# Hybrid encoder trunk, two layers: sums of squares as two rounded passes, and where squares and up-projection lifts stand

## The reference

```
h = rms_norm(x);  p = h @ W_in
A: 4 heads, two softmax maps each, RMS norm of every 64-wide q and k, partial rotary,
   w = softmax1 - lam * softmax2;  o = rms_norm(w @ v, subln_w) * (1 - lambda_init)
B: 4 q heads, 2 kv heads of 128, RMS norm of q and k, axial rotary
C: latent attention: cq (384) and ckv (256) normed, projected up to q (128 + 64 rotary per head),
   k (128 per head) and v; norms of q and k parts; one rotary key kr (64) shared by the heads
D: 4 pooling windows minus token, per-group linear, scale
y = concat(A, B, C, D) * silu(gates);  x = x + y @ W_out
```

## Time and profile before

| | us |
|---|---|
| median of 3 runs | 913.04 (912.84 to 913.1) |
| the profiled execution | 912.77 |
| its span in the trace | 911.0 |
| PE busy | 899.7 (99%) |
| DVE busy | 637.0 (70%) |
| ACT busy | 585.5 (64%) |

### The profile page before, as it was taken

The page is one execution under the profiler, slowest core; times in us unless marked ns, Lnnn a source line. Parts: engine busy times, 40 slices in busy tenths (PEclk is TensorE's granted clock), DMA queues, the critical chain, the costliest instruction groups (busy, mean ns, idle before and its releaser), DMA issues.

```text
span 911.0 us, 18111 instructions
## 1 busy us (share of the span) xinstructions
PE 899.7 (99%) x7054; PEld 858.4 (94%) x7054; DVE 637.0 (70%) x1071; ACT 585.5 (64%) x1045; POOL 0.2 (0%) x4
## 2 busy tenths in 40 slices
PE   8999999999999999999999999999999999999998
PEld 7998998999999999999999989999999999999998
DVE  7785887768777776766665658876687667666552
ACT  7678756678666667745554588566686666675331
POOL 0000000000000000000000000000000000000000
PEclk9999999999999999999999999999999999999999
DMA  8654343343444343445455544334425344445562
GB/s 332 260 188 142 134 142 132 109 139 129 140 141 142 138 148 128 145 149 192 166 195 185 186 155 169 119 119 161 158 93 186 128 151 145 149 171 185 187 201 78
DMA packets 22997, 143.83 MB, mean 158 GB/s; under 512 B 2560, under 2 KB 4736, under 8 KB 6528
## 3 DMA queue, kind: packets, MB, share of 16 engines
q1 hardware_dynamic: 22768, 142.64, 44.0%
q10 hardware_dynamic: 144, 0.04, 0.0%
HBM read 140.57 MB, written 2.10 MB: 157 GB/s over the span
## 4 chain that ended last, share of the span: by engine, by line
PE 89%; ACT 7%; DVE 2%; issue 1%; DMA 1%; SPq 0%; ACTq 0%; DVEq 0%
PE dense L725 25%; PE dense L727 24%; PE dense L726 24%; PE s_ps L889 4%; PE o_ps L924 4%; ACT w_hi L1014 2%; PE norm_ps L845 2%; PE t_ps L905 2%; DVE w_lo L1319 1%; ACT qw L1087 1%; DMA x<-xt_dram 1%; PE swap_ps L860 0%; ACT sq L1084 0%; PE norm_ps L727 0%; PE swap_ps L727 0%
## 5 line engine op out<-in xcount | busy, mean ns | idle before, releaser
L725 PE MATMUL dense<-h_hi,w_hi 128*128 128x272 f32 (+2 forms) x1440 | 427.1, 297 | 1.5 <-DVE h_lo L1299 0.9
L727 PE MATMUL dense<-h_hi,w_lo 128*128 128x272 f32 (+2 forms) x1440 | 412.6, 287 | 0.0
L726 PE MATMUL dense<-h_lo,w_hi 128*128 128x272 f32 (+2 forms) x1440 | 410.6, 285 | 0.0
L1319 DVE TENSOR_TENSOR w_lo<-raw,w_hi 128x1024 fp32r<-128x1024 f32 (+1 forms) x257 | 313.3, 1219 | 88.4 <-ACT w_hi L1014 82.3
L1014 ACT ACTIVATE w_hi<-raw 128x1024 fp32r<-128x1024 f32 (+1 forms) x257 | 271.3, 1056 | 68.7 <-PE dense L727 53.9
L725 PEld LDWEIGHTS dense<-h_hi,w_hi 128*128 128x128 f32 x1440 | 271.3, 188 | 8.2 <-issue 3.8
L726 PEld LDWEIGHTS dense<-h_lo,w_hi 128*128 128x128 f32 x1440 | 271.5, 189 | 1.3
L727 PEld LDWEIGHTS dense<-h_hi,w_lo 128*128 128x128 f32 x1440 | 271.1, 188 | 0.0
L725 PE MATMUL dense<-y_hi,w_hi 128*128 128x272 f32 (+1 forms) x500 | 143.1, 286 | 2.3 <-ACT q_st L1059 1.3
L727 PE MATMUL dense<-y_hi,w_lo 128*128 128x272 f32 (+1 forms) x500 | 142.7, 285 | 0.0
L726 PE MATMUL dense<-y_lo,w_hi 128*128 128x272 f32 (+1 forms) x500 | 142.4, 285 | 0.0
(11 more groups left out here) (161 smaller groups left out, 813.4 us busy)
## 6 DMA issues: line engine op xcount, KB each, us to landing
raw<-w_stream_dram SPq DMA_DIRECT2D x128, 1024.0 KB, 4.8
out_dram<-x SPq DMA_DIRECT2D x8, 256.0 KB, 6.3
x<-xt_dram SPq DMA_DIRECT2D x3, 544.0 KB, 8.9
raw<-w_stream_dram SPq DMA_DIRECT2D x3, 512.0 KB, 7.5
con<-consts_dram SPq DMA_DIRECT2D x1, 984.0 KB, 7.4
x<-xt_dram SPq DMA_DIRECT2D x2, 272.0 KB, 4.8
raw<-w_stream_dram SPq DMA_DIRECT2D x2, 256.0 KB, 4.6
d_w<-consts_dram SPq DMA_DIRECT2D x2, 256.0 KB, 5.1
```

The source lines that it names most:

```text
L725: nc.tensor.matmul(ps, whi, xhi, start=first, stop=False)
L726: nc.tensor.matmul(ps, whi, xlo, start=False, stop=False)
L727: return nc.tensor.matmul(ps, wlo, xhi, start=False, stop=last)
L1319: signal(nc.vector.tensor_tensor(w_lo[:, g % RING, 0:n], raw[:, e % RAW, CHUNK * half:CHUNK * half + n], w_hi[:, g % RING, 0:n].bitcast(F3 ...
```

## The change

It does six things.

1. The sums of rope_stat and sub_stat are made as two fp32r matmuls (`two`) into the same bank, of a rounded tile sq_hi and of what the rounding leaves, sq_lo, with rounded copies of the two tables (ones and blocks, exact in them; made once on ACT).
2. For a single tile ACT writes sq_hi as a third instruction of rope_pre or a second of sub_pre, and DVE gets a new stage sq_low (one subtraction). For a pair, DVE's sq_sum gets two more instructions, a copy (CAST) and a subtraction. PE waits for DVE's `summed` in every case.
3. For single tiles of aq and ak, for kr and for the sub norm, the sum and what follows it stand a slot later. Pairs' sums keep their slot, as do those of qr; kr's squares stand a slot later too. sub_slot avoids the slots in which A's and B's sums now stand.
4. On ACT rope_pre goes from 0.11 to 0.62 of the slot, behind p_out (0.56) and the lifts (0.6); on DVE the sums of pairs go from 0.2 to 0.64, behind pool, s_scale and rescale.
5. Up-projection tiles are lifted as stages of their own: the second tiles of the first three up chunks come behind the next split (up_next, 0.715), and the split of chunk 18 is pulled nearly a slot forward by `MOVED`, ahead of the rounding of the latent (y_hi).
6. Some small stores change place (eps, one, lambda and its sums, in stat, v_st; the sub weights in par), and stat is used with fewer columns.

```diff
 AT_SCALAR = dict(rope_fin=-0.166, ..., sub_fin=0.1, rope_pre=0.62,
...
+                 lift=0.6, up_out=0.705, up_next=0.715, split=0.71, x_square=0.72, y_gate=0.73, y_lat=0.74, ...)
+AT_VECTOR = dict(sq_sum=0.64, sq_low=0.64, lat_sum=0.2, rope_mid=0.25, ...
...
+MOVED = {..., **{("split", l, 18): -0.98 for l in range(DEPTH)},
...
                 if kind in ("aq", "ak"):
                     at(s, ("rope_pre", l, kind, i0 + j, j))
-                    at(s, ("rope_stat", l, kind, i0 + j))
-                    at(s + 1, ("rope_fin", l, kind, i0 + j))
+                    at(s, ("sq_low", "rope", l, kind, i0 + j))
+                    at(s + 1, ("rope_stat", l, kind, i0 + j))
+                    at(s + 2, ("rope_fin", l, kind, i0 + j))
...
-        at(s + 8, ("rope_pre", l, "kr", 0, None))
-        at(s + 9, ("rope_stat", l, "kr", 0))
-        at(s + 10, ("rope_fin", l, "kr", 0))
+        at(s + 9, ("rope_pre", l, "kr", 0, None))
+        at(s + 9, ("sq_low", "rope", l, "kr", 0))
+        at(s + 10, ("rope_stat", l, "kr", 0))
+        at(s + 11, ("rope_fin", l, "kr", 0))
...
-            at(s + 4 + c, ("up_out", l, c))
+            for j in range(UP_TILES[c]):
+                at(s + 4 + c, ("up_next" if c < 3 and j else "up_out", l, c, j))
...
-                at(s, ("sub_stat", l, n))
-                at(s + 1, ("sub_fin", l, n))
-                at(s + 1, ("y_split", "sub_fin", l, n))
+                at(s, ("sq_low", "sub", l, n))
+                at(s + 1, ("sub_stat", l, n))
+                at(s + 2, ("sub_fin", l, n))
+                at(s + 2, ("y_split", "sub_fin", l, n))
...
+        def two(ps, table, hi, lo):
+            nc.tensor.matmul(ps, table, hi, start=True, stop=False)
+            return nc.tensor.matmul(ps, table, lo, start=False, stop=True)
...
         def rope_stat(l, key, i):
-            if key in PAIRED:
-                pe.wait_ge(summed, sum_no[("rope", l, key, i)])
-            else:
-                pe.wait_ge(pre_done, pre_no[("rope_pre", l, key, i)])
+            pe.wait_ge(summed, sum_no[("rope", l, key, i)])
             norm_free("rope_stat", l, key, i)
-            sums = nc.tensor.matmul(norm_ps[:, t0:L], halves, sq[:, 2 * parity("rope_stat", l, key, i), t0:L],
-                                    start=True, stop=True)
+            half = parity("rope_stat", l, key, i)
+            sums = two(norm_ps[:, t0:L], halves_r, sq_hi[:, half, t0:L], sq_lo[:, half, t0:L])
...
         def rope_pre(l, key, i, j):
...
+            link(nc.scalar.activation(sq[:, 2 * half, t0:L], src, ACT.Square))
+            link(nc.scalar.activation(qw[:, half, t0:L], src, ACT.Copy, scale=pcol(l, key)))
+            signal(nc.scalar.activation(sq_hi[:, half, t0:L], sq[:, 2 * half, t0:L], ACT.Copy),
+                   pre_done, pre_no[("rope_pre", l, key, i)])
...
         def sq_sum(what, l, key, i=None):
...
-            signal(nc.vector.tensor_tensor(a, a, b, ALU.add), summed, n)
+            link(nc.vector.tensor_tensor(a, a, b, ALU.add))
+            high = sq_hi[:, half, t0:L]
+            link(nc.vector.tensor_copy(high, a))
+            signal(nc.vector.tensor_tensor(sq_lo[:, half, t0:L], a, high.bitcast(F32), ALU.subtract), summed, n)
+
+        def sq_low(what, *of):
...
+            signal(nc.vector.tensor_tensor(sq_lo[:, half, t0:L], sq[:, 2 * half, t0:L],
+                                           sq_hi[:, half, t0:L].bitcast(F32), ALU.subtract), summed,
+                   sum_no[(what, *of)])
```

More of the change, by code:

```diff
@@ L215, in make_plan @@
             at(s, ("rope_pre", l, key, i, None))
-            if key in PAIRED:
-                at(s, ("sq_sum", "rope", l, key, i))
+            at(s, ("sq_sum" if key in PAIRED else "sq_low", "rope", l, key, i))
             at(s + 1, ("rope_stat", l, key, i))
@@ L289, in build @@
     sq = sb("sq", [128, 4, L])
+    sums_of = sb("sums_of", [128, 256], F32R)
+    sq_hi = sb("sq_hi", [128, 2, L], F32R)
+    sq_lo = sb("sq_lo", [128, 2, L], F32R)
     qw = sb("qw", [128, 2, L])
@@ L303, in build @@
     lam_in = v_st[:, 0, 0:DEPTH * 256]
-    lam_sum = sb("lam_sum", [128, DEPTH * 2])
-    neg_lam = sb("neg_lam", [128, DEPTH])
-    sub_w = sb("sub_w", [128, DEPTH])
-    eps_c = sb("eps_c", [128, 1])
-    one_c = sb("one_c", [128, 1])
+    lam_sum = v_st[:, 1, 0:DEPTH * 2]
+    neg_lam, eps_c, one_c = stat[:, 2:2 + DEPTH], stat[:, 6:7], stat[:, 7:8]
     dense = [bank("dense0"), bank("dense1")]
@@ L914, in pv @@
             if branch == "c":
-                pe.wait_ge(up_taken, UP_TILES * (l + 1))
+                pe.wait_ge(up_taken, sum(UP_TILES) * (l + 1))
             else:
@@ L928, in sub_stat @@
         def sub_stat(l, n):
-            pe.wait_ge(pre_done, pre_no[("sub_pre", l, n)])
+            pe.wait_ge(summed, sum_no[("sub", l, n)])
             norm_free("sub_stat", l, n)
             t0 = first_query(l)
-            nc.tensor.matmul(norm_ps[:, t0:L], ones, sq[:, 2 * parity("sub_stat", l, n), t0:L],
-                             start=True, stop=True).then_inc(stat_done, 1)
+            half = parity("sub_stat", l, n)
+            two(norm_ps[:, t0:L], ones_r, sq_hi[:, half, t0:L], sq_lo[:, half, t0:L]).then_inc(stat_done, 1)
         run = dict(setup=warm_up, chunk=chunk, xsum=xsum, rope_stat=rope_stat, lat_stat=lat_stat, v_turn=v_turn, mix=mix,
@@ L985, in lambda_exp @@
             signal(nc.scalar.activation(lam_sum[:, :], lam_sum[:, :], ACT.Exp), lam_exp, 1)
+            act.wait_ge(s_const, 16)
+            nc.scalar.activation(sums_of[:, :], con[:, CC["ones"]:CC["ones"] + 256], ACT.Copy).then_inc(ones_ready, 1)
         def x_tile(l, kt):
@@ L1104, in sub_pre @@
             buffers_free("sub_stat", l, n)
-            signal(nc.scalar.activation(sq[:, 2 * parity("sub_stat", l, n), t0:L], o_ps[:, t0:L], ACT.Square), pre_done,
+            half = parity("sub_stat", l, n)
+            link(nc.scalar.activation(sq[:, 2 * half, t0:L], o_ps[:, t0:L], ACT.Square))
+            signal(nc.scalar.activation(sq_hi[:, half, t0:L], sq[:, 2 * half, t0:L], ACT.Copy), pre_done,
                    pre_no[("sub_pre", l, n)])
@@ L1182, in s_exp @@
                 signal(nc.scalar.activation(probs[0:nq, k % 2, m, :], s_ps[m][0:nq, 0:L], ACT.Exp,
[L1183 removed]
+                                            bias=stat[0:nq, m:m + 1], scale=SCALE[b],
                                             accum_out=stat[0:nq, 4 + m:5 + m]), exp_done, 2 * k + m + 1)
```

94 lines of the change are left out of this document (48 added, 46 removed).

## The result

The changed kernel takes 917.59 us (median of 6 runs, 916.92 to 917.82) against 912.94 for the kernel before (6 runs, 912.7 to 913.11): ratio 1.005, 95% interval 1.004 to 1.006. It is slower by 4.6 us where 909.7 was forecast, and lies outside the range.

A forecast was written before the change was run, and what follows sets the result against it. PE, busy 899.7 of 911.0 us, was taken as the bound. 912.77 less 9.1 for cheaper sums, less 7.2 for waits that go, plus 13.0 for waits that come gave 909.5 (909.7 as median), range 901 to 916.5.

The forecast's parts named there:

- The sums' price: On PE, two rounded passes take 0.252 us instead of 0.454 per sum; 44 sums save 9.1 us.
- The waits that go: PE's 11 waits on late ACT instructions, such as up-projection lifts and p_t copies, vanish with their restarts, saving 7.2 us.
- The three places: Three least-margin places where PE would newly wait on longer DVE and ACT chains: 2.7, 3.4 and 4.3 us.
- kn1: Second latent key pair (slot 30.6): its sum comes late behind the softmax's scale, 1.6 and 1.8 us, together 3.4.
- head 1: Differential head 1's product with the values waits for o_ps, held by the sub norm's last step: 1.8 and 2.5 us.
- kn0: First latent key pair (slot 24.6): its sum waits for DVE's subtraction, 1.1 and 1.6 us, together 2.7.
- Waits that come: New PE waits, since every sum now waits for DVE, which like ACT works in order: 13.0 us, bounds 4 and 19.
- "smaller" places: Margins under 0.5 us: query rope sum, c2's turn (0.3 a layer each), B's query pairs 0.8, late lifts 0.6; 2.6 us.
- The first (few waits): Rival: the new waits mostly don't come, as ACT and DVE have 30% spare; 4.5 us of waits, 901.2; 22%.
- the second: Rival: DVE falls behind on w_lo in the lead-in and differential heads, so dense chunks wait; 916; 16%.
- The third (passes no cheaper): Rival: a weight reload or switch eats the two passes' 0.20 us on PE; without the 9.1, 918.8; 4%.
- something else: Remaining rival: a clock that drops in a longer stall, or an order misread; mostly slower; 6%.

The follow-up runs named there:

- e1: Kernel before with only the up-projection's part: its tiles lifted as stages of their own, chunk 18's split pulled forward; 911.15 us (0.9979).
- e12: e1 with kr's square and scaled copy on ACT moved behind v_st's lifts; 911.97 us (0.9989).
- e9: Changed kernel's order of stages with the arithmetic of the kernel before: one fp32 sum, nothing added on ACT or DVE; 911.30 us (0.9981).
- e5: Changed kernel with the sub norm's last step, which frees o_ps, moved on DVE ahead of two rescales and s_max; 923.92 us (1.0114).
- e2: Changed kernel with each sum one fp32 matmul; ACT and DVE still make sq_hi and sq_lo, and PE waits for them; 920.03 us (1.0077).
- e13: e9 plus ACT's part of the addition alone: 30 copies to sq_hi that nobody reads; 913.01 us (1.0001).
- e14: e9 plus DVE's part alone: 30 subtractions, and copy and subtraction for 14 pairs, with PE waiting for DVE; 918.0 us (1.0055).
- e4: Changed kernel with squares on ACT back at 0.11 of the slot and head tiles' sums on DVE back at 0.2; 913.88 us (1.0013).
- e6: Changed kernel with kr's squares, sum and rotation one slot earlier, its squares just behind v_st's lifts; 918.03 us (1.0055).
- e18: Changed kernel with squares back at 0.11, head tiles' sums at 0.2, and sq_hi and sq_lo of all 44 sums made on GpSimd; 910.18 us (0.9966).

## Why the prediction was wrong, point by point

- **The sums' price** was right (0.25 for 0.454 us). **The waits that go** went, all of the up-projection, row and qw; p_t shrank, probs grew. In the two up-projections PE gained 3.0 us where 3.4 had been counted (six waits with 0.16 each, less 0.6). e1 and e12 show that some 40% of it came not with the lifts but with kr's later square.
- **The three places** were right in the size of the idle times, and kn1 and head 1 also in what is waited for. kn1: 1.59 and 1.70 us (forecast 1.6 and 1.8). Head 1: 1.70 and 2.25 (1.8 and 2.5). Around kn0: 1.56 and 2.03 (1.4 and 1.9 with qr), but there the forecast named another wait. It said that kn0's sum waits for DVE's sq_lo, 1.1 and 1.6 us; that wait is 0.21 and 0.41. The long ones, 0.91 and 1.33, are qn0's sum waiting for ACT's rn of kr, which stands behind a gate and a split. The forecast has this rn in its chain, but not that qn0's sum needs norm_ps, which rn frees. The DVE chain that it adds up, 12.8 us from v_st's last lift, is there (13.2, from 74.54 to 87.74) and ends just behind PE, because PE has already stood for rn. That the sizes agree is in part luck.
- **The step that failed is the term "Waits that come", 13.0 us.** Without its 0.6 for lifts it was 12.4; the runs show 15.0 us of idle time, which cost PE 19.0 us. (a) I priced a wait that goes with its restart but a wait that comes without. After PE stood, its next row comes late and the one behind it too (in the changed kernel, 0.91 us of idle time made 82.89 to 84.08, then 84.28, where 0.126 is usual: 0.16 and 0.07). On the average of the 16 waits it is 0.25, 4.0 us in all, but not at each: at kn1 the chunk is 1.43 and 1.55 us longer, the sum's saving added back, for 1.59 and 1.70 of idle time. (b) The "smaller" places were not small: c2's turn 2.1 for 0.6 (two waits of o_ps on yt in C, both in layer 1), B's pairs 1.35 for 0.8, p_t and probs 0.7 for nothing; the three places 0.1 under forecast.
- **Where the 8.0 us between forecast (909.5) and result (917.4) of the profiled executions lie**, by distances between the same chunks of the two traces, with 0.20 added back for each sum: around kn0 5.8 for 3.3, kn1 3.0 for 3.4, head 1 4.9 for 4.3, c2's turn 2.2 for 0.6, B's pairs 1.9 for 0.8, p_t and probs 1.2 for nothing. These are the 19.0 for 12.4, 6.6 of the 8.0. The up-projections add 0.4, mostly short stops like that at 528.39. The first chunks add 0.4; e1, e9 and e12 have 0.2 to 0.5 there too, so it is not the change's. The sums saved 8.9 for 9.1, and 0.4 to 0.5 us are left.
- **Behind it stands a premise that the experiments overturn**: that work on DVE and ACT is hidden unless it ends at one of a few places. From e9 on, 13 us of ACT cost 1.7, 23.6 of DVE 6.7, and 13.2 more of DVE 5.8 (4.6 without the clock). On average DVE is busy for 72% in the changed kernel; in the heads and the lead-in it has no gap over 0.15 us but one of 0.23 from 79.79 to 102.64, and none from 211.53 to 228.44. In the kernel before, it still stood 0.4 to 1.1 us four times between 80 and 91. I read the traces so that ACT and DVE hand each other the delay there (s_max, exponentials, square, sum, rotation), and PE follows; e5 shows one such case. So much of the saving on PE upstream of such a place isn't saved: of e2's 9.0 us the changed kernel gets 2.4.
- **The rivals.** The first (few waits) is refuted. In the second the time (916) was near, but not its mechanism: no dense matmul waited for w_lo behind the first chunks; the delay came at sums and o_ps. The third (passes no cheaper) was wrong in what it said of the passes; that its time, 918.8, was nearest is chance. The clock, named among "something else", was 1.00 in the changed kernel's profile.
- **The account by parts**: order -1.8 (e9), ACT and DVE's additions +8.7 (e2 over e9), two passes -2.4, together +4.5, for 4.6 measured. The parts are steps from one run to the next, so that they add up says nothing by itself; what supports them is that e13 and e14, made each for itself, give 8.4 of the 8.7.

## What to carry to other kernels

Where an engine is at 99%, don't price its helpers by their mean load: walk the chain between two of its fixed points and see whether the helper has any gap there; if not, each instruction added to it costs a part of itself (here 0.13 us per us on ACT, 0.28 to 0.35 on DVE, 0.44 with the clock), and much of a saving on the full engine upstream is waited away (here 39 to 73%). Price a new wait with its restart, just as the one that goes, and compare chunk by chunk: a list of waits leaves out the short ones. Look at the granted clock of every execution before two medians are compared. Test an order without the arithmetic that came with it, and before repairing the place where the wait shows, ask which loop it belongs to: of four such repairs (e4, e5, e6, e12) one helped, two only moved it (0.4 and 0.8 us slower), and one made it worse by 5 to 6 us. A control is missing for e18: the fp32 sums in e4's order, so what that order gives by itself is known only with the added work.
